# Four u tiles worked between the query blocks of the gathered tokens

## The reference

```python
q = (xt @ wq).reshape(T, PEER_HEADS, 2, PEER_HALF).astype(jnp.float32)      # 8 heads, 2 halves of 128
s = jnp.einsum('thpd,hpnd->thpn', q, keys.astype(jnp.float32))              # 128 keys each
ts, ti = lax.top_k(s, PEER_TOPK)                                            # 16 best of each list
cand_s = (ts[:, :, 0, :, None] + ts[:, :, 1, None, :]).reshape(T, PEER_HEADS, PEER_TOPK * PEER_TOPK)
best_s, pos = lax.top_k(cand_s, PEER_TOPK)                                  # 16 experts of each head
gate = jax.nn.softmax(best_s, axis=-1).astype(xn.dtype)
...
hu = jnp.einsum('chkd,cd->chk', jnp.take(u, ib, axis=0), xb)
act = jax.nn.gelu(hu, approximate=False) * gb
return jnp.einsum('chk,chkd->cd', act, jnp.take(v, ib, axis=0))
```

## Time and profile before

| | |
|---|---|
| median of 3 runs | 1928.57 us (1928.20 to 1937.28) |
| time of the profiled execution | 1927.72 us |
| its span, first to last instruction | 1925.9 us |
| busy PE, DVE, ACT, POOL | 1649.8, 1455.9, 752.5, 669.5 us |
| chain that ended last | PE 57%, DVE 32%, issue 5%, ACT 3%, DMA 2% |

### The profile page before, as it was taken

The page is one execution under the profiler, slowest core; times in us unless marked ns, Lnnn a source line. Parts: engine busy times, 40 slices in busy tenths (PEclk is TensorE's granted clock), DMA queues, the critical chain, the costliest instruction groups (busy, mean ns, idle before and its releaser), DMA issues.

```text
span 1925.9 us, 22943 instructions
## 1 busy us (share of the span) xinstructions
PE 1649.8 (86%) x8237; PEld 1441.1 (75%) x8237; DVE 1455.9 (76%) x2648; ACT 752.5 (39%) x1243; POOL 669.5 (35%) x517
## 2 busy tenths in 40 slices
PE   4995434688969999899979998999999999999997
PEld 3774323466869777799979998999878778777876
DVE  2429884312777799977789999997689789888986
ACT  1121111210234222244477887886333333333332
POOL 0049920000001133311146666665244334444440
PEclk8998655899979999999989998999999999999999
DMA  4210500011437587777779999999999999999995
GB/s 162 66 45 22 58 0 1 11 44 55 165 96 243 181 290 272 235 238 234 235 261 393 394 396 378 389 399 395 349 377 391 337 376 385 377 372 383 386 338 191
DMA packets 162199, 477.43 MB, mean 248 GB/s; under 512 B 27823, under 2 KB 61295, under 8 KB 159783
## 3 DMA queue, kind: packets, MB, share of 16 engines
q1 hardware_dynamic: 106791, 274.62, 41.2%
q0 software_dynamic: 55296, 201.35, 27.7%
HBM read 420.93 MB, written 54.42 MB: 247 GB/s over the span
## 4 chain that ended last, share of the span: by engine, by line
PE 57%; DVE 32%; issue 5%; ACT 3%; DMA 2%; DVEq 0%; SPq 0%; ACTq 0%
PE ps L732 22%; PE ps L660 16%; PE ps L503 9%; DVE ring L1273 7%; DVE cacc L1379 4%; DVE lo L1158 3%; PE ps L710 2%; PE ps L513 2%; DVE gA L1320 2%; DVE gB L1320 2%; DVE acc L1277 2%; DVE tsi L1173 2%; DVE tsi L1170 2%; DVE sm L1171 2%; DVE tsv L1172 1%
## 5 line engine op out<-in xcount | busy, mean ns | idle before, releaser
L1004 POOL DMA_INDIRECT ring<-in_u,idx x192 | 270.0, 1406 | 733.7 <-DVE hu L1273 354.4
L1158 DVE TENSOR_TENSOR lo<-raw,hi 128x1024 fp32r<-128x1024 f32 x256 | 313.4, 1224 | 142.6 <-ACT hi L861 138.1
L861 ACT ACTIVATE hi<-raw 128x1024 fp32r<-128x1024 f32 x256 | 270.4, 1057 | 325.2 <-PE ps L732 321.7
L1004 POOL DMA_INDIRECT ring<-in_v,idx x192 | 273.0, 1422 | 356.9 <-DVE acc L1277 343.0
L660 PE MATMUL ps<-xh,hi 128*128 128x384 f32 x1024 | 357.8, 349 | 27.2 <-DVE lo L1158 27.2
L660 PE MATMUL ps<-xl,hi 128*128 128x384 f32 x1024 | 349.2, 341 | 0.0
L660 PE MATMUL ps<-xh,lo 128*128 128x384 f32 x1024 | 348.5, 340 | 0.0
L732 PE MATMUL ps<-hi,ah 128*128 128x512 f32 x768 | 239.5, 393 | 18.5 <-DVE al L1350 18.2
L1277 DVE SCALAR_TENSOR_TENSOR acc<-ring,hu,acc 128x1024 f32<-128x1024 f32 x192 | 245.7, 1280 | 1.6
L732 PE MATMUL ps<-lo,ah 128*128 128x512 f32 x768 | 239.0, 393 | 0.0
L732 PE MATMUL ps<-hi,al 128*128 128x512 f32 x768 | 238.4, 392 | 0.0
(11 more groups left out here) (175 smaller groups left out, 2069.5 us busy)
## 6 DMA issues: line engine op xcount, KB each, us to landing
raw<-in_uT SPq DMA_DIRECT2D x128, 512.0 KB
raw<-in_v SPq DMA_DIRECT2D x128, 512.0 KB
wring<-in_wblk SPq DMA_DIRECT2D x56, 512.0 KB
gelu_matrix<-gest SPq DMA_DIRECT2D x64, 384.0 KB
gate_matrix<-Gs SPq DMA_DIRECT2D x16, 1536.0 KB
Gl<-gate_matrix SPq DMA_DIRECT2D x128, 192.0 KB
gel<-gelu_matrix SPq DMA_DIRECT2D x128, 192.0 KB
ring<-in_u,idx POOLq DMA_INDIRECT x192
```

Source lines behind the costliest of these rows:

```text
L861: nc.scalar.activation(hi[:, s % 2, :], raw[:, s % RAWS, :], ACT.Copy).then_inc(s_hi, 1)
L1004: pool.indirect_dma_start(ring[:, r % SLOTS, :], None, table, bass.IndirectOffsetOnAxis(idx[:, t, c:c + 1], 0)).then_inc(g_in[r % SLOTS], 16)
L1158: nc.vector.tensor_tensor(lo[:, s % 2, :], raw[:, s % RAWS, :], hi[:, s % 2, :].bitcast(F32), ALU.subtract).then_inc(s_lo, 1)
```

## The change

The first four u tiles (`U_FIRST = 4`) move from the stretch of the picks into the first ranking. PE works u tile 0, 1, 2, 3 in the rounds 7, 9, 11, 13, behind the score block of the round before (`U_AT`). DVE works their `low` behind the ranks of rounds 5, 7, 9 and 11. ACT does `high(0)` in round 3, `high(1)` in round 5, and `step(0)` to `step(3)` in rounds 8, 10, 12 and 14. So that `ps[3]` is free for the u tiles, all score blocks of the first ranking go to the pair 2, by turns to its two halves; each still waits until the scores of two rounds before have been copied out. The split into `xh` and `xl` goes at two pieces to a round, and is over after four rounds. The picks now carry 7 and 7 calls of `low` instead of 8 and 9 (and one ahead of them). The numbers in the tables shift with it. From `wqb0` on the order of every engine is as before.

```diff
+U_FIRST = 4
 U_TOP = 17
...
+U_AT = {7 + 2 * n: n for n in range(U_FIRST)}
+ROWS_AFTER = {5: TA, 7: TB}
+EXP_AFTER = {8: TA, 15: TB, 39: 0, 51: 1, 63: 2}
+KEYS_AFTER = {10: TB, 33: 0, 45: 1, 57: 2}
...
         if m:
-            plan += [(f"sca{m - 1}", 2 + (m - 1) % 2)]
-    plan += [(f"sca{NM - 1}", 3)]
+            plan += [(f"sca{m - 1}", 2)]
+    plan += [(f"sca{NM - 1}", 2)]
...
                 load_block(NMIX + RING + m)
-            for n in range(U_TOP):
+                if m in U_AT:
+                    after_u(U_AT[m])
+            for n in range(U_FIRST, U_TOP):
                 after_u(n)
...
+                if kind == "a":
+                    pe.wait_ge(F[2], use[f"sca{m}"][1] - (2 if m else 1))
+                    out, ready = ps[2][:, (m % 2) * 512:], R[2]
+                else:
+                    out, ready = take(f"sc{kind}{m}")
...
                 queries(f"wqa{m}", DT, GT)
                 if m:
                     scores("a", m - 1, (TA, TB))
+                if m in U_AT:
+                    if U_AT[m] == 0:
+                        pe.wait_ge(s_xl, DC)
+                        pe.wait_ge(F[3], use["ms2"][1])
+                    dense_u(U_AT[m])
             scores("a", NM - 1, (TA, TB))
 
-            pe.wait_ge(s_xl, DC)
-            pe.wait_ge(F[3], use[f"sca{NM - 1}"][1])
-            for n in range(U_TOP):
+            for n in range(U_FIRST, U_TOP):
                 dense_u(n)
...
                 if m:
                     score_out("a", m - 1)
+                if m in (3, 5):
+                    high((m - 3) // 2)
+                if m - 1 in U_AT:
+                    step(U_AT[m - 1])
             score_out("a", NM - 1)
-            high(0)
-            high(1)
             expand_keys(TA)
-            for n in range(U_TOP):
+            for n in range(U_FIRST, U_TOP):
                 step(n)
...
             for m in range(NM):
-                if m < DC:
-                    x_low(m)
+                for c in range(2 * m, min(2 * m + 2, DC)):
+                    x_low(c)
                 key_ranks("a", m, (TA, TB))
+                if m + 2 in U_AT:
+                    low(U_AT[m + 2])
...
-            low(0)
-            picks(TA, 0, range(1, 9))
-            picks(TB, 1, range(9, U_TOP + 1))
+            picks(TA, 0, range(U_FIRST, 11))
+            picks(TB, 1, range(11, U_TOP + 1))
```

More of the change, by code:

```diff
@@ L86 @@
 RANKED = (TA, TB, 0, 1, 2)
-ROWS_AFTER = {2: TA, 4: TB}
-EXP_AFTER = {5: TA, 13: TB, 39: 0, 51: 1, 63: 2}
-KEYS_AFTER = {8: TB, 33: 0, 45: 1, 57: 2}
+U_AT = {7 + 2 * n: n for n in range(U_FIRST)}
+ROWS_AFTER = {5: TA, 7: TB}
+EXP_AFTER = {8: TA, 15: TB, 39: 0, 51: 1, 63: 2}
+KEYS_AFTER = {10: TB, 33: 0, 45: 1, 57: 2}
 GELU_AFTER = {29: 0, 56: 1}
@@ L636, in scores @@
                 pe.wait_ge(F[pair], n)
-                out, ready = take(f"sc{kind}{m}")
+                if kind == "a":
[3 more added lines that the diff above has]
+                    out, ready = take(f"sc{kind}{m}")
                 for i, t in enumerate(tiles):
@@ L851, in score_out @@
                 if kind == "a":
+                    p = p[:, (m % 2) * 512:]
                     nc.scalar.activation(sm[:, m % 2, 0, :], p[:, 0:P], ACT.Copy)
@@ L902, in _ @@
                 query_out(f"wqa{m}", m, DT, GT, f"sca{m - 2}" if m >= 2 else None)
-                if m < DC:
-                    act.wait_ge(s_xn2, m + 1)
-                    nc.scalar.activation(xh[:, m, :], xn[:, m, 0:DT], ACT.Copy).then_inc(s_xh, 1)
+                for c in range(2 * m, min(2 * m + 2, DC)):
+                    act.wait_ge(s_xn2, c + 1)
+                    nc.scalar.activation(xh[:, c, :], xn[:, c, 0:DT], ACT.Copy).then_inc(s_xh, 1)
                 if m:
                     score_out("a", m - 1)
+                if m in (3, 5):
+                    high((m - 3) // 2)
+                if m - 1 in U_AT:
+                    step(U_AT[m - 1])
             score_out("a", NM - 1)
-            high(0)
-            high(1)
             expand_keys(TA)
-            for n in range(U_TOP):
+            for n in range(U_FIRST, U_TOP):
                 step(n)
```

## The result

The changed kernel took 1947.38 us in the median of 11 runs (1940.66 to 1959.84), the kernel before 1928.57 us. The ratio is 1.0083, with a 95% interval of 1.0063 to 1.0103: slower by some 16 us, 12 to 20. The two medians lie 18.8 us apart, which is within that interval. The profiled execution took 1950.6 us, its span was 1948.8 us against 1925.9.

What follows compares the result with a forecast made beforehand. DVE was taken to pace the first ranking and PE's tile 15 the picks. Terms 27.8 - 16.6 - 2.8 + 5.1 + 1.7 gave +15.2 us, so a median of 1943.8 us, range 1936 to 1951.

Steps and rivals of the forecast that it cites:

- tile 0 starts; its length: First ranking, PE: u tile 0 waits 7.0 us for `low(0)`, starts at 520.4, takes 6.8 us at half clock.
- ranks of rounds 7, 9, 11, 13: First ranking, DVE: these ranks start at 531.2, 544.5, 557.8 and 571.1, in loops of 13.3 us for two rounds.
- waits of DVE: First ranking: DVE waits 7.3 us before round 7, then 4.6 us in each of three loops, 21.1 us in all.
- TA's `keyf`; tile 4: Start of the picks: `keyf` at 582.8, 24.1 us later; tile 4 at 586.7, 27.8 us later than tile 0 before.
- wait at the change to TB; loss by half clock behind it: Picks, PE ahead of tile 11: a wait of 5.1 us in place of 2.80, then 1.7 us lost to half clock.
- TB's `keyf`: Picks, DVE: TB's picks start at 621.7, behind `low(10)`, the multiplication, and the sums and ends.
- scores of the second ranking: Behind PE's tile 15, `wqb0` and `wqb1`: scores start near 658.5, with tile 15 ending 15.2 us later.
- from there to the gates: From the second ranking's scores on: the same length as before, since no order changed from `wqb0` on.
- Starving of DVE: First ranking: PE's tiles wait for DVE's `low` and hold back scores, so DVE waits 21.1 us.
- The PSUM pair at nothing: First ranking: scores in the halves of one PSUM pair cost nothing, or at most 1.28 us, one round's handover.
- every wait drops the clock: Rival, 6%: the 2.4 us waits ahead of tiles 1 to 3 halve the clock too, giving +23.0, 1951.6 us.
- A start that stays late: From `wqb0` to the end: a later start stays a later end, so +15.2 us carries through.

Runs made afterwards that it cites:

- early_low: Changed kernel with each of its four `low` two rounds earlier on DVE; ratio to the kernel before 0.9987 (0.9960 to 1.0014).
- two_tiles: Changed kernel with only u tiles 0 and 1 in the first ranking; second ranking 160.3 us behind the first scores (changed kernel 166.4), no ratio.
- no_tiles: Changed kernel without u tiles in the first ranking, `low(0)` and lists as in the kernel before; ratio to that kernel 0.9996 (0.9975 to 1.0017).
- six_early: Changed kernel with `low` of tiles 0 to 3 earlier, tiles 4 and 5 behind the first ranking's last scores; median 1923.8 us, ratio to before 0.9970.
- filled_wait: Changed kernel plus 40 unused matmuls in PE's wait ahead of tile 0; second ranking 165.6 us behind the first scores (changed kernel 166.4), no ratio.
- lists_8_6: Changed kernel with `low(11)` moved from TB's list to TA's; second ranking 164.4 us behind the first scores (changed kernel 166.4), no ratio.
- six_early_b: six_early executed once more, unchanged; ratio to the kernel before 0.9942 (0.9918 to 0.9965).

## Why the prediction was right

Forecast were 1943.8 us on a median of 1928.6, +15.2, with a range of 1936 to 1951; measured are 1947.38 us and a ratio of 1.0083, +16.0 with 12 to 20. The steps, by place in the span:

| step | forecast | measured |
|---|---|---|
| tile 0 starts; its length | 520.4; 6.8 | 520.96; 7.0 |
| ranks of rounds 7, 9, 11, 13 | 531.2, 544.5, 557.8, 571.1 | 531.8, 546.6, 560.1, 573.3 |
| waits of DVE | 7.3 and 3 x 4.6 | 7.5, 6.2, 4.7, 4.7 |
| TA's `keyf`; tile 4 | 582.8; 586.7 | 585.0; 588.8 |
| wait at the change to TB; loss by half clock behind it | 5.1; 1.7 | 4.89; 1.6 |
| TB's `keyf` | 621.7 | 622.5 |
| scores of the second ranking | 658.5 | 659.0 |
| from there to the gates | as before | as before, to 0.1 us |

**Starving of DVE** is shown. It goes when only the place of `low` is changed (early_low), grows by the tile (two_tiles), and is absent without the tiles (no_tiles).

**The PSUM pair at nothing** is shown by no_tiles.

**Two terms were off, and against each other,** so that the sum came out nearer than its parts, which is luck. DVE's second wait was 6.2 instead of 4.6 us, because the clock halved for 3.4 us from 537.3 on, behind a PE wait of 2.16 us that I had put at no loss. The rival that every wait drops the clock held for one of the three waits it named. The Trainium skill (TensorE: Matmul & The Clock Gate, section "HAM oscillation") tells of a loop whose wait puts the array back to the half clock in every round, and its rule is for waits longer than the three here. The trace agrees for the waits of 2.51 and 2.15 us, behind which the clock stayed, and not for the one of 2.16. On the other side tile 4 was not as slow as tile 0 before: from 588.79 tiles 4 and 5 took 9.9 us to 598.66, so tile 4 5.7 and not 6.8. A smaller one: `low(0)` was taken to start where round 6 had started, 26.65 us behind the first scores, and started at 27.06, since all eight pieces of `xl` now stand ahead of it and seven did before. Together that made +2.2 us at `keyf` and +0.5 us at the second ranking.

**A start that stays late.** Up to the gates this is shown for every kernel here but the two runs of six_early: 325.1 to 325.4 us. Behind them a single profile doesn't tell. The v stage took 556.4, 559.0 and 563.1 us where the order was that of before, and 568.2 and 564.8 in the changed kernel. But filled_wait and lists_8_6, which start it as late, have 561.7 and 561.4, and six_early and six_early_b, one kernel, have 566.4 and 557.0. So the 11.8 us more of the changed kernel's profile can be drift. Whether some 3 us of them belong to it stays open: no run holds that stage alone against the other, and +15.6 with 3 more is still within the 12 to 20 of the ratio.

## What to carry to other kernels

Before work is moved into an engine's idle time, ask who waits for what stands behind it in that engine's queue: here PE's tile stood ahead of the scores that DVE, the slower engine of the stage, needed next, and itself waited for a piece that DVE did late. A loop of that kind costs its whole way round, here 13.2 to 13.5 us for 8.6 us of DVE's work. If the slower engine makes the moved piece's input earlier, while it still has finished scores to work on, the loop opens. Then the idle time that was to be used must still be looked for, since here it lay behind the last scores and not between the blocks.

## What the runs showed of the hardware

A wait of PE of 2.16 us, ahead of tile 1, was followed by 3.4 us at half clock, and the longer ones of 2.51 and 2.80 us, ahead of tile 2 and at the change to TB before, were not. The wait of 2.79 us at the change to TB in lists_8_6, as long as the one before to 0.01 us, was followed by 3.4 us at half. The wait of 11.88 us was followed by 3.1 us of half clock in the changed kernel (588.8 to 591.9) and by 6.0 us in filled_wait. So the length of a wait alone did not tell its price: at that place it differed by some 1.5 us between two programs.

The v stage of one and the same program differed by 9.4 us between two executions (566.4 and 557.0), while the stages up to the gates repeated to 0.3 us. PE's waits for DVE in it, of six_early and then of six_early_b:

```profile
PE ps L744 <- DVE al L1365: 23.6, 8, 4.0
```

```profile
PE ps L744 <- DVE al L1365: 20.1, 8, 3.2
```

(1356 to 1927 us, and 1351 to 1914 us). The first of the eight stands ahead of the stage; without it they are 20.4 and 17.5 us, 2.9 us apart. Behind seven of the eight waits 3.4 us at half clock followed in six_early, 23.9 us in all, and in six_early_b only 10.2 us of the stage were at half (1628.5 to 1635.3 and 1700.2 to 1703.6). By an estimate that takes half of these stretches as lost, that is 12.0 and 5.1 us, 6.9 us apart. The two differences together are 9.8 us, against the 9.4 measured. In all twelve profiles the stage up to its last matmul, less PE's idle time and half of the time at half clock, is 522.8 to 524.2 us. So what differs between executions there is PE's idle time and the clock; why the waits differ is open.
